# Weight buffers 64 bytes further on in SBUF, activations in place

## Chip, cores and metric

One core of one Trainium2 chip. The metric is the time of one execution on the device in microseconds. "Faster" and "slower" compare medians of several executions.

## What is computed

The reference runs two transformer blocks on a sequence of 512 tokens with a model width of 1024, all in float32.

```python
# first block (16 meta tokens ahead of the 512)
z = rms(h) @ w_in                     # 1024 x 7168: q, k, v, glu, two gates
o = differential attention of 8 heads, block-causal mask
u = silu(layernorm(causal depthwise conv of 31 taps(glu gated)))
m = sigmoid(g_att) * y_att + sigmoid(g_conv) * (u @ w_conv_out)
h = h + m @ w_out
h = h + (silu(gate) * val) @ w_down   # gate, val = conv3(rms(h) @ w_up), 2 x 2816 wide
# second block, two layers
proj = rms(x) @ w_in_2[layer]         # 1024 x 8192
mix  = [gated conv branch (1024), retention of 8 heads (1024)]
x = x + rms(mix @ w_out_2[layer])     # 2048 x 1024
```

Nearly all the arithmetic is matrix products of a weight matrix with the activations.

## The kernel before

Activations live transposed in SBUF: 128 channels on the partitions, tokens along the free axis, one slice for each of the 8 (`KT`) groups of 128 channels. Weights come from memory in chunks of 256 (`CW`) output columns: one chunk is 8 slices of 128 x 256 float32, 1 MB. Two buffers of each kind take turns (`j` = 0, 1).

To keep the accuracy of float32 with operands in the format float32r, every product is made of three. A chunk lands in `raw[j]` (SyncE's `load`, line 257). ScalarE copies it to `w_hi[j]`, rounded (`hi`, line 865). VectorE writes the rest, `raw - w_hi`, to `w_lo[j]` (`lo`, line 1228). The activations have such a pair too: `n_hi`/`n_lo`, `m_hi`/`m_lo`, `u_lo`, `s_hi`/`s_lo`, `x_hi`/`x_lo`. Then TensorE adds up w_hi * x_lo, w_hi * x_hi and w_lo * x_hi over the 8 slices in PSUM.

`tile` (line 390) issues this for 128 output columns. Its matmul (line 406) has the weight slice `w[j][:, k, jj*128:(jj+1)*128]` as stationary operand and the activations as moving operand. With 512 tokens that is one matmul; with more (`T1` = 528 tokens with the meta tokens, `T2` = 514 of them) it is two pieces, 256 columns into one bank and the rest (272 or 258) into the other. The argument `c0` is the column at which the moving operand begins: 0, or `OLD` = 14 where the first block drops 14 of the meta tokens (two groups of projections in the attention stretch, the convolution gate). Each piece loads its weights anew.

In two places the roles are turned, since there tokens are wanted on the partitions. `v_block` (line 509) makes the value of the attention: the stationary operand is a slice of 128 tokens of `n_hi` or `n_lo` that begins at column 16 + 128 q (a fifth block takes columns 0 to 16), the moving operand is `w[0][:, k, :]`, 256 columns (line 520). `head_pair` does the same for the retention: the stationary operand is `s_hi` or `s_lo` from column 128 q, the moving one again `w[0][:, k, :]` (line 751). The first chunk of each retention layer is issued at line 734.

The order of all work is written out by hand for each engine and held together by semaphores. TensorE's order alternates chunks 0 and 1; `lo_full[j]` releases it, and `acc_full` releases ScalarE to overwrite `w_hi[j]`. In the attention stretch slices of later projections (`fill`) are put between the steps of the softmax. TensorE has matmuls of plain float32 as well: scores, transposes through `ident`, the retention sums (line 787).

SBUF tensors are laid out in the order in which the program declares them, each beginning at a multiple of 32 bytes in its partition; those of inner scopes share the bytes behind. The first is `raw0` at byte 16512. The places before the change:

| tensor | byte | modulo 128 | modulo 256 |
|---|---|---|---|
| raw0, raw1 | 16512, 24704 | 0 | 128 |
| w_hi0, w_hi1 | 32896, 41088 | 0 | 128 |
| w_lo0, w_lo1 | 49280, 57472 | 0 | 128 |
| h, par, ident | 65664, 82560, 85120 | 0 | 128 |
| n_hi, n_lo (rows of 2304 bytes) | 101504, 119936 | 0 | 128 |
| m_hi, m_lo (rows of 2304 bytes) | 138368, 156800 | 0 | 128 |
| s_hi, s_lo (rows of 2048 bytes) | 101504, 117888 | 0 | 128 |
| x_hi, x_lo (rows of 2048 bytes) | 134272, 167040 | 0 | 128 |

Of the kernel before, what the change touches and what calls it, by code (L numbers as in the profile page):

```python
# [24 lines left out]
P = 128  # L25
# [62 lines left out]
def build(nc, io, out):  # L88
# [14 lines left out]
    with ctx:  # L103
        def sb(name, shape, dt=fp32, at=None):
            return (at or ctx).enter_context(nc.sbuf_tensor(name, shape, dt))
# [2 lines left out]
            return ctx.enter_context(nc.semaphore(name))  # L108


        raw = [sb(f"raw{j}", [P, KT, CW]) for j in range(2)]
        w_hi = [sb(f"w_hi{j}", [P, KT, CW], f32r) for j in range(2)]
        w_lo = [sb(f"w_lo{j}", [P, KT, CW], f32r) for j in range(2)]
# [22 lines left out]
        head_ms = sb("head_ms", [P, UNITS])  # L136
        lams = sb("lams", [1, 4])
        sub_w = sb("sub_w", [P, 1])
        sb("to_the_phase_of_w", [P, 32])


        area = ExitStack()
# [1719 lines left out]
```

## Time and profile before

| | us |
|---|---|
| median of 3 runs (lowest, highest) | 1958.2 (1957.84, 1959.83) |
| profiled execution | 1962.2 |
| its span, first to last instruction | 1960.4 |
| mean granted TensorE clock | 0.982 |

The profile divides the span into 40 slices of 49 us. The first lines are the busy shares in tenths, then the clock granted to TensorE, and the bandwidth moved:

```profile
PE   6999999999999999999899999999989999999998
DVE  6677897886546546566575554444256555544422
ACT  4224454355333323234422222222232222222222
PEclk7999999999999999999899999999989999999999
DMA  4221111112223222222322323232322323232321
```

PE is TensorE (matmuls), PEld its weight loads, DVE VectorE, ACT ScalarE. The first 45 us are start and first normalisation; the GLU projections run to 152, the attention to 441, the output projections and the feed-forward network to 950, the two retention layers to 1445 and 1940. A matmul's duration in the profile is longer than the distance from its start to the next one's, since matmuls are pipelined.

### The profile page before, as it was taken

How to read it: one execution, taken by the hardware profiler on the slowest of the kernel's cores; microseconds unless marked ns; L12 is line 12 of the kernel's file. 1: busy time of each engine (PE TensorE's matmuls, PEld its weight loads, DVE VectorE, ACT ScalarE, POOL GpSimd, SP SyncE). 2: the span in 40 equal slices, each digit the busy share in tenths (PEclk: the TensorE clock that was granted, in tenths of full speed). 3: DMA queues.
4: the chain of work that ended last, by engine and by line, in shares of the span. 5: the costliest groups of instructions: out<-in, count | busy, mean ns of one | idle time of the engine just before them, and what ended most of it. 6: DMA issues, size and time to landing. Idle time of an engine off the chain costs nothing.

```text
span 1960.4 us, 29930 instructions
## 1 busy us (share of the span) xinstructions
PE 1906.9 (97%) x11809; PEld 1694.7 (86%) x11809; DVE 1142.0 (58%) x1516; ACT 627.5 (32%) x1060; POOL 72.8 (4%) x69
## 2 busy tenths in 40 slices
PE   6999999999999999999899999999989999999998
PEld 5998888889999999899788888888878888888887
DVE  6677897886546546566575554444256555544422
ACT  4224454355333323234422222222232222222222
POOL 2000100110000000000000000000000000000000
PEclk7999999999999999999899999999989999999999
DMA  4221111112223222222322323232322323232321
GB/s 133 89 87 64 65 43 64 64 50 79 87 90 103 80 93 95 98 86 65 97 72 90 94 78 106 87 97 96 106 75 67 94 78 96 86 107 86 104 90 43
DMA packets 159216, 165.86 MB, mean 85 GB/s; under 512 B 2968, under 2 KB 156065, under 8 KB 159154
## 3 DMA queue, kind: packets, MB, share of 16 engines
q1 hardware_dynamic: 156648, 160.73, 26.3%
q10 hardware_dynamic: 2186, 4.20, 0.6%
q8 instruction: 44, 0.72, 0.2%
q14 instruction: 18, 0.15, 0.0%
q0 software_dynamic: 320, 0.07, 0.0%
HBM read 162.88 MB, written 2.10 MB: 84 GB/s over the span
## 4 chain that ended last, share of the span: by engine, by line
issue 50%; PE 41%; DVE 6%; POOL 1%; ACT 1%; DMA 0%; DVEq 0%; POOLq 0%; ACTq 0%
PE acc L406 29%; PE acc L520 3%; PE acc L734 2%; PE acc L751 2%; DVE y L1312 1%; PE tr L787 1%; PE sc L562 1%; DVE ssum L1698 1%; PE sc L773 1%; DVE w_lo L1228 1%; POOL pw L347 0%; PE tr L593 0%; DVE ssum L1276 0%; PE tr L440 0%; PE tr L591 0%
## 5 line engine op out<-in xcount | busy, mean ns | idle before, releaser
L1228 DVE TENSOR_TENSOR w_lo<-raw,w_hi 128x2048 fp32r<-128x2048 f32 x148 | 338.7, 2289 | 157.7 <-ACT w_hi L865 156.2
L865 ACT ACTIVATE w_hi<-raw 128x2048 fp32r<-128x2048 f32 x147 | 280.8, 1910 | 447.9 <-PE acc L406 432.8
L406 PE MATMUL acc<-s_lo,w_hi 128*128 128x512 f32 x848 | 333.0, 393 | 0.0
L406 PE MATMUL acc<-s_hi,w_lo 128*128 128x512 f32 x848 | 330.3, 389 | 0.0
L406 PE MATMUL acc<-s_hi,w_hi 128*128 128x512 f32 x848 | 330.1, 389 | 0.0
L406 PE MATMUL acc<-n_lo,w_hi 128*128 128x256 f32 (+3 forms) x1072 | 259.9, 310 | 6.1 <-DVE n_lo L1256 3.1
L406 PE MATMUL acc<-n_hi,w_hi 128*128 128x256 f32 (+3 forms) x1072 | 250.8, 302 | 0.0
L406 PE MATMUL acc<-n_hi,w_lo 128*128 128x256 f32 (+3 forms) x1072 | 250.6, 302 | 0.0
L406 PEld LDWEIGHTS acc<-n_lo,w_hi 128*128 128x128 f32 x1072 | 172.8, 190 | 29.0 <-issue 16.7
L406 PEld LDWEIGHTS acc<-s_hi,w_lo 128*128 128x128 f32 x848 | 159.2, 188 | 33.2
L406 PEld LDWEIGHTS acc<-s_lo,w_hi 128*128 128x128 f32 x848 | 159.3, 188 | 32.1
L406 PEld LDWEIGHTS acc<-s_hi,w_hi 128*128 128x128 f32 x848 | 159.3, 188 | 32.0
L406 PEld LDWEIGHTS acc<-n_hi,w_lo 128*128 128x128 f32 x1072 | 173.9, 190 | 6.9
L406 PEld LDWEIGHTS acc<-n_hi,w_hi 128*128 128x128 f32 x1072 | 173.8, 190 | 6.6
L406 PE MATMUL acc<-m_hi,w_hi 128*128 128x256 f32 x832 | 167.9, 283 | 0.0
L406 PE MATMUL acc<-m_hi,w_lo 128*128 128x256 f32 x832 | 167.8, 283 | 0.0
L1312 DVE SCALAR_TENSOR_TENSOR y<-u,par,y (+1 forms) x240 | 164.5, 747 | 1.7 <-DVE neg_lam L1361 0.4
L406 PE MATMUL acc<-m_lo,w_hi 128*128 128x256 f32 x704 | 143.5, 285 | 0.8 <-DVE h L1525 0.2
L406 PEld LDWEIGHTS acc<-m_hi,w_lo 128*128 128x128 f32 x832 | 129.1, 190 | 0.0
L406 PEld LDWEIGHTS acc<-m_hi,w_hi 128*128 128x128 f32 x832 | 129.0, 190 | 0.0
L406 PEld LDWEIGHTS acc<-m_lo,w_hi 128*128 128x128 f32 x704 | 109.1, 190 | 3.9 <-DVE z L1545 2.4
L406 PE MATMUL acc<-x_hi,w_lo 128*128 128x512 f32 x256 | 99.6, 389 | 0.0
(274 smaller groups left out, 2619.7 us busy)
## 6 DMA issues: line engine op xcount, KB each, us to landing
raw<-in_w_in SPq DMA_DIRECT2D x92, 1024.0 KB, 5.8
raw<-in_w_up SPq DMA_DIRECT2D x22, 1024.0 KB, 5.1
raw<-in_w_out SPq DMA_DIRECT2D x20, 1024.0 KB, 5.2
raw<-in_w_down SPq DMA_DIRECT2D x8, 1024.0 KB, 5.1
raw<-in_w_conv_out SPq DMA_DIRECT2D x4, 1024.0 KB, 5.3
decay<-in_decay ACTq DMA_DIRECT2D x8, 512.0 KB, 5.3
raw<-in_w_down SPq DMA_DIRECT2D x4, 768.0 KB, 4.8
xs<-in_x SPq DMA_DIRECT2D x4, 512.0 KB, 5.2
```

The source lines that it names most:

```text
L406: last = pe.matmul(acc[jj][:, bank, at_:at_ + n], w[j][:, k, jj * P:(jj + 1) * P], x[:, k0 + k, c:c + n], start=start and k == 0 and p == ...
L520: last = pe.matmul(dst, x[:, k, c:c + m], w[0][:, k, :], start=k == 0 and p == 0, stop=k == KT - 1 and p == 2)
L562: last = pe.matmul(sc[:, m, 0:keys], qs, kT[part, hh, 0:keys], start=True, stop=True)
L734: last = pe.matmul(acc[jj][:, j, :], w[j][:, k, jj * P:(jj + 1) * P], x[:, k, :], start=k == 0 and w is w_hi and x is s_hi, stop=k == KT - ...
L751: last = pe.matmul(acc[jj][:, 0, (q % 2) * CW:(q % 2 + 1) * CW], x[:, k, q * P:(q + 1) * P], w[0][:, k, :], start=k == 0 and p == 0, stop= ...
L773: last = pe.matmul(dst, rk[:, hh, kb * P:(kb + 1) * P], rq[:, hh, kb * P:SEQ], start=True, stop=True)
L787: last = pe.matmul(dst[:, q * P:(q + 1) * P], st[:, c:c + P], rv[:, kb, hh * P:(hh + 1) * P], start=kb == 0, stop=kb == q)
L865: act.activation(w_hi[j][:, :, :], raw[j][:, :, :], ACT.Copy).then_inc(hi_full[j], 1)
L1228: dve.tensor_tensor(w_lo[j][:, :, :], raw[j][:, :, :], w_hi[j][:, :, :].bitcast(fp32), ALU.subtract).then_inc(lo_full[j], 1)
L1312: dve.scalar_tensor_tensor(out=dst, in0=src, scalar=w, in1=dst, op0=ALU.mult, op1=ALU.add).then_inc(s["conv"], 1)
L1698: dve.tensor_reduce(ssum[:, 0:SEQ], h2[:, :, :].rearrange("p t n -> p n t"), AX.X, ALU.add).then_inc(s["hsum"], 1)
```

## The change

A tensor `lead` of 16 floats (64 bytes in each partition) is declared ahead of `raw`, and the pad that stood after `sub_w`, 32 floats, is replaced by one of 16. Neither is read or written. All tensors from `raw0` to `sub_w` move up by 64 bytes; the weight buffers then begin at 64 modulo 128 (192 modulo 256). `n_hi` and everything declared after it stay at their bytes. No instruction is added, taken away or moved.

```diff
+        sb("lead", [P, 16])
         raw = [sb(f"raw{j}", [P, KT, CW]) for j in range(2)]
         w_hi = [sb(f"w_hi{j}", [P, KT, CW], f32r) for j in range(2)]
         w_lo = [sb(f"w_lo{j}", [P, KT, CW], f32r) for j in range(2)]
...
         sub_w = sb("sub_w", [P, 1])
-        sb("to_the_phase_of_w", [P, 32])
+        sb("to_the_phase_of_x", [P, 16])
```

## Rows read from the trace of the kernel before

**Rows 1.** The page: busy us, share of the span, instructions of each engine.

```profile
PE 1906.9 (97%) x11809; PEld 1694.7 (86%) x11809; DVE 1142.0 (58%) x1516; ACT 627.5 (32%) x1060; POOL 72.8 (4%) x69
```

**Rows 2.** Busy time by stage: stretch, length, then each engine's busy us.

```profile
45.00:152.00 107.00, 106.41 (x865) 105.62 (x866) 77.49 (x98) 23.44 (x19) 0.00 (x0) 1.00 0.30 98
152.00:441.00 289.00, 282.24 (x2228) 251.16 (x2228) 236.94 (x454) 136.01 (x444) 34.30 (x12) 1.00 0.17 56
441.00:950.00 509.00, 504.40 (x3669) 478.82 (x3669) 299.59 (x353) 183.63 (x201) 4.82 (x2) 0.99 0.28 89
1000.00:1445.00 445.00, 444.46 (x2184) 373.60 (x2182) 210.07 (x241) 115.77 (x165) 7.35 (x8) 1.00 0.31 93
```

**Rows 3.** Chain that ended last, 1600 to 1960: start, us, what, count.

```profile
1646.47 11.51 PE acc L751 x96
...
1684.04 255.70 PE acc L406 x1128
```

**Rows 4.** Timeline of TensorE, feed-forward, first and last of 37 rows.

```profile
893.12 0.40 PE L406 MATMUL acc<-m_lo,w_hi 128*128 128x256 f32 x2
...
901.76 0.40 PE L406 MATMUL acc<-m_lo,w_hi 128*128 128x256 f32 x2
```

**Rows 5.** Timeline of TensorE, GLU, width T1, first and last of 25 rows.

```profile
59.97 0.41 PE L406 MATMUL acc<-n_hi,w_lo 128*128 128x256 f32 x2
...
65.83 0.40 PE L406 MATMUL acc<-n_hi,w_lo 128*128 128x256 f32 x2
```

**Rows 6.** Timeline of TensorE, from column 14, first and last of 38 rows.

```profile
129.93 0.40 PE L406 MATMUL acc<-n_hi,w_hi 128*128 128x256 f32 x2
...
138.81 0.40 PE L406 MATMUL acc<-n_hi,w_lo 128*128 128x256 f32 x2
```

**Rows 7.** Timeline of TensorE, line 520, first and last of 13 rows.

```profile
156.75 0.28 PE L520 MATMUL acc<-w_hi,n_hi 128*128 128x256 f32 x1
...
158.11 0.28 PE L520 MATMUL acc<-w_hi,n_hi 128*128 128x256 f32 x1
```

**Rows 8.** Groups of matmuls by shape: count, busy us, mean ns of one.

```profile
L406 PE MATMUL acc<-s_hi,w_lo 128*128 128x512 f32 x848 | 330.3, 389 | 0.0
...
L406 PE MATMUL acc<-m_hi,w_hi 128*128 128x258 f32 x416 | 117.3, 282 | 0.0
...
L406 PE MATMUL acc<-x_hi,w_lo 128*128 128x512 f32 x256 | 99.6, 389 | 0.0
...
L406 PE MATMUL acc<-m_lo,w_hi 128*128 128x258 f32 x352 | 99.3, 282 | 0.0
...
L751 PE MATMUL acc<-w_hi,s_hi 128*128 128x256 f32 x256 | 73.6, 288 | 0.0
...
L406 PE MATMUL acc<-n_hi,w_hi 128*128 128x512 f32 x176 | 68.5, 389 | 0.0
...
L406 PE MATMUL acc<-n_hi,w_hi 128*128 128x258 f32 x240 | 68.5, 285 | 0.0
...
L406 PE MATMUL acc<-n_hi,w_hi 128*128 128x272 f32 x208 | 60.1, 289 | 0.0
...
L520 PE MATMUL acc<-w_hi,n_hi 128*128 128x256 f32 x128 | 35.4, 277 | 0.0
...
L406 PE MATMUL acc<-u_lo,w_hi 128*128 128x258 f32 x64 | 18.0, 282 | 0.0
...
L520 PE MATMUL acc<-w_hi,n_hi 128*16 128x256 f32 x32 | 8.8, 276 | 0.0
```

**Rows 9.** The page's groups and DMA issues: mean ns, us to landing.

```profile
L1228 DVE TENSOR_TENSOR w_lo<-raw,w_hi 128x2048 fp32r<-128x2048 f32 x148 | 338.7, 2289 | 157.7 <-ACT w_hi L865 156.2
L865 ACT ACTIVATE w_hi<-raw 128x2048 fp32r<-128x2048 f32 x147 | 280.8, 1910 | 447.9 <-PE acc L406 432.8
...
raw<-in_w_in SPq DMA_DIRECT2D x92, 1024.0 KB, 5.8
```

**Rows 10.** Who waited for whom: us in total, times, longest.

```profile
ACT w_hi L865 <- PE acc L406: 432.8, 71, 10.8
```

## The prediction, made before the changed kernel was run

> **What bounds the kernel now.** I read the busy shares first [rows 1]: TensorE has matmuls in flight for 1906.9 of 1960.4 us. Only 53.5 us of the span are without one. The table by stage [rows 2] says the same more sharply: between 1000 and 1445 us TensorE is busy for 444.46 of 445 us while VectorE is busy for 210 and ScalarE for 116. The second retention layer repeats this. The feed-forward stretch (441 to 950) stands at 504.4 of 509, the GLU stretch (45 to 152) at 106.4 of 107. Only in the attention stretch (152 to 441) does VectorE come near, with 236.9 of 289. So the time of this kernel is the number of matmuls times their pace, and any edit that leaves the pace alone is worth little.
>
> The change adds no instruction, no wait and no transfer. It moves addresses. The question is therefore whether the pace of a matmul depends on where its operands begin, and the trace holds a natural experiment on that.
>
> **The pace, read from the trace.** The durations that the profile gives a matmul overlap their neighbours; the pace is the distance between starts. At a granted clock of 1.00 (the 2.4 GHz level) 512 columns stream in 213.3 ns and 256 in 106.7 ns. What lies above is paid per matmul:
> - 512 columns, weights stationary: 255.70 us for 1128 matmuls, 226.7 ns each [rows 3], 13.4 ns above.
> - Pieces of 256 and 258 over `m_hi`/`m_lo`: 36 pairs from 893.12 to 901.76, 240.0 ns a pair [rows 4]. Streaming is 214.2, so 12.9 ns above for each matmul.
> - Pieces of 256 and 272 over `n_hi`/`n_lo` (width T1): 24 pairs from 59.97 to 65.83, 244.2 ns a pair, streaming 220.0, so 12.1 each [rows 5].
> - Pieces of 256 and 258 over `n_hi`/`n_lo` that begin at column 14, 56 bytes in: 37 pairs from 129.93 to 138.81, 240.0 ns, 12.9 each [rows 6].
> - Line 751 (the retention value, activation slice stationary, weights moving, 256 columns): 11.51 us for 96, 119.9 ns, 13.2 above [rows 3].
> - Line 520 (the attention value, again activation slice stationary, weights moving, 256 columns): 12 steps from 156.75 to 158.11, 113.3 ns, 6.6 above [rows 7].
>
> The last two are the same matmul in shape and in moving operand (`w_hi[0]`, `w_lo[0]`). What differs is the stationary slice. Line 751 takes `s_hi[:, k, q*128:...]`, whose byte address is a multiple of 128. Line 520 takes `n_hi[:, k, 16+q*128:...]`: the META offset of 16 floats puts it 64 bytes past a multiple of 128. Every weight slice of line 406 is at present a multiple of 128 (`w_hi0` is at byte 32896 = 257*128, slices step by 512) and so is every activation tensor it streams, except where column 14 is added. So all matmuls with a stationary operand at phase 0 pay about 13 ns, and the one group with the stationary operand at phase 64 and the moving one at phase 0 pays half. After the change line 406 has just that arrangement, in absolute bytes too: stationary at 192 modulo 256, moving at 128 modulo 256.
>
> Two things in the rows weaken this. The 16-column loads of line 520 (fifth block, columns 0 to 16) begin at phase 0 and its matmuls show the same duration as the 128-column ones, 276 against 277 ns [rows 8]; a short load may simply be free, but it may also be that `n` as stationary operand is cheap for another reason: its rows are 2304 bytes apart, those of `s` 2048. And a moving operand 56 bytes in [rows 6] gains nothing over one at 0, although its distance to the weights is then nearly 64 as well. So it may be the phase of the stationary operand alone that counts.
>
> The Trainium skill speaks against any effect. Its page "TensorE: Matmul & The Clock Gate", section "Step-by-step: what each phase is for", says that TensorE has two independent read ports of SBUF and that loading the next tile's weights takes no bandwidth from the running matmul; by that a shift of 64 bytes changes nothing and the time stays. Rows 3 against rows 7, 119.9 against 113.3 ns for one shape, are not explained by it.
>
> **The change part by part.** Moving `lead` in ahead of `raw0` and shrinking the pad after `sub_w` from 128 to 64 bytes moves raw, `w_hi`, `w_lo`, `h`, `par`, `ident`, the statistics tiles and `pw` up by 64 bytes. `n_hi` stays at byte 101504, with everything behind it.
>
> (a) Line 406 and weights at phase 64, activations at phase 0. With 512 columns: 3 passes of 848, 256 and 176 matmuls [rows 8], together 3840, each from 13.4 to 6.6 above streaming, 6.8 ns: 26.1 us. Pieces of 256/258 from column 0: over `m` 416+416+352 pairs, over `u_lo` 64, over `n` in the output projection 2*2*2*8 = 64 for each of three passes, together 1440 pairs or 2880 matmuls, 6.3 ns each: 18.1 us. Width T1: 208 pairs in each of three passes [rows 8], 1248 matmuls, from 12.1 to 6.6, 5.5 ns: 6.9 us. Sum 51.1 us. The 144 matmuls of line 734 are left out (1.0 us).
>
> (b) Pieces from column 14: 240-64 = 176 pairs a pass, 1056 matmuls. Stationary 64, moving 56. If the stationary phase alone counts, 6.3 ns each, a gain of 6.7 us; if the distance counts, they stay about equal, 0.
>
> (c) Line 520: stationary stays at 64, moving goes to 64. 384 matmuls with 128-column loads [rows 8]. 0, or a loss of 6.6 ns each, 2.5 us.
>
> (d) Line 751: stationary stays at 0, moving goes to 64. 768 matmuls [rows 8]. 0, or a gain of 6.6 ns each, 5.1 us.
>
> (b) to (d) come as one of two sets: +6.7 for "stationary phase", +2.6 for "distance". I take the middle, 4.6, and keep both ends. Gross 55.7 us.
>
> (e) What does not pass through. In the attention stretch the matmuls between the softmax steps are filler, and VectorE is busy 82% of it. The gain there is 384 matmuls of width T1 (2.1 us) and up to 768 from column 14 (4.8 us); I count half of it lost, 2 us. At the start of the kernel, at the two layer starts and at its end the saved time of a few matmuls meets a chain of statistics that is no shorter; I take 2.5 us. Net 51 us.
>
> (f) The weight path. A 1 MB load lands in 5.8 us, is copied by ScalarE in 1.91 and split by VectorE in 2.29 us [rows 9]. A chunk of 48 matmuls of 512 columns lasts 48*226.7 = 10.9 us, or 10.6 after, and the two conversions take 4.2 of it, the load having landed a chunk earlier. The copy waits for TensorE for 432.8 us in all [rows 10], so it is early, not late. Its cover holds: were the load to take twice as long for its new phase, or both conversions 10% more (0.4 us), nothing of it would show. Their operands all move together, so I take 0. If that cover were gone, 0.4 us for each of 147 chunks would be 59 us.
>
> (g) float32 matmuls (transposes, scores) keep stream and operands, apart from `ident`, `nf` and `rb`, which move 64 bytes; 0, with an end of 2 us either way.
>
> **The sum.** The profiled execution took 1962.2 us (span 1960.4). 1962.2-51 = 1911.2. The median of the runs is 4.0 us under the profiled one, so the forecast is 1907 us.
>
> **The rivals.** (1) No effect: the 113.3 ns of line 520 belong to the pitch of `n` or to its role, not to its phase. Then the time is 1958, within a microsecond or two. For it: the 16-column loads, the 56-byte rows and the port rule. (2) Only 256-column matmuls gain, since only those were seen fast; with 512 columns the pace stays at 226.7. Then (a) is 18.1+6.9 = 25.0 us, with 4.6 from (b) to (d) and 4.5 lost in (e) 25.1 net: 1933. (3) Slower: a 512-byte weight slice from a multiple of 128 covers four blocks of 128 bytes, from 64 past it five. If each block read costs a pause, 13.4 ns at four is 3.35 a block, and the fifth adds 3.35 ns to 7968+1056 = 9024 matmuls: 30 us, 1988. It decides from the point where line 520, whose slices lie across five blocks already, owes its pace to something else that hides the fifth; its 113.3 ns speaks against this directly.
>
> **How the numbers follow.** The likeliest case 0.66; no effect 0.17; half 0.06; slower 0.11. The likeliest case's own range is 1896 to 1925: its low end takes all of +6.7, no loss in (e) and (g) for it (1958.2-51.1-6.7-1.0-2 = 1897, and one more for the reading of the paces), its high end lets three fifths of the gross 55.7 through (33). To leave out no more than 2 in 10 the range must also take in the no-effect case, so 1896 to 1961. About 0.2% (4 us) is what a measurement of this kernel can tell from no change. Faster 0.72, same 0.17, slower 0.11.
>
> **What would show it.** In the changed kernel the long run of line 406 at the end should show 1128 matmuls in about 248 us (219.9 ns each), a pair over `m` about 227.4 ns. If lines 520 and 751 keep 113.3 and 119.9 while the column-14 pairs fall to 227, the stationary phase counts; if 520 rises to 120 and 751 falls to 113, the distance does. If the pace of line 406 stays at 226.7, the prediction is wrong at its root, and nothing else in the kernel could bring 50 us. If the pace falls but the time does not, the waits on VectorE's `w_lo` and softmax tiles should have grown.

## The result: slower, and the working part of the forecast had the wrong sign

| | before | after |
|---|---|---|
| median of 3 runs (lowest, highest), us | 1958.2 (1957.84, 1959.83) | 1975.94 (1975.91, 1978.34) |
| profiled execution, us | 1962.2 | 1978.34 |
| its span, us | 1960.4 | 1976.5 |
| mean granted TensorE clock | 0.982 | 0.985 |

The ratio after/before is 1.0089, 95% interval 1.0074 to 1.0103. The forecast was 1907 us in a range of 1896 to 1961. The kernel did not get 51 us shorter, it got 18 us longer.

### The profile after

The busy line of the changed kernel's page:

```profile
PE 1923.3 (97%) x11809; PEld 1686.5 (85%) x11809; DVE 1141.9 (58%) x1516; ACT 627.7 (32%) x1060; POOL 72.7 (4%) x69
```

Against [rows 1] the instruction counts are the same on every engine. VectorE, ScalarE and GpSimd are busy for the same time within 0.2 us. TensorE alone changed: 1906.9 to 1923.3 us, 16.4 more, where the span grew by 16.1 (its weight loads, PEld, which run beside the matmuls, are busy 8.2 us less). Its mean granted clock is no lower, 0.985 against 0.982. So no wait was added; the matmuls themselves come at another pace.

The busy time by stage, to be laid beside [rows 2] (stretch, length, then each engine's busy us, granted clock, DMA share, GB/s):

```profile
45.00:152.00 107.00, 106.50 (x878) 105.72 (x879) 78.48 (x100) 25.23 (x22) 0.00 (x0) 1.00 0.30 99
152.00:444.00 292.00, 284.85 (x2227) 253.68 (x2227) 237.12 (x452) 135.82 (x443) 34.26 (x12) 1.00 0.18 58
444.00:950.00 506.00, 500.32 (x3662) 471.71 (x3661) 299.31 (x354) 183.67 (x202) 4.82 (x2) 0.99 0.28 90
1007.00:1455.00 448.00, 446.15 (x2146) 367.06 (x2145) 207.33 (x238) 114.94 (x164) 8.05 (x9) 1.00 0.30 90
```

The GLU stretch holds 878 matmuls in 107 us where it held 865: a little faster. The retention stretch holds 2146 in 448 us where it held 2184 in 445: slower. The two signs live in one kernel, and what separates them is the width of the matmul.

The chain that ended last gives the two long runs that answer to [rows 3]:

```profile
1654.72 11.31 PE acc L752 x96
...
1692.49 263.19 PE acc L407 x1128
```

Lines are one higher than before (line 406 is now 407). The 1128 matmuls of 512 columns take 263.19 us instead of 255.70: 233.3 ns each instead of 226.7. The forecast wanted 248. The 96 matmuls of the retention value take 11.31 instead of 11.51: 117.8 ns instead of 119.9.

The narrow ones, from TensorE's timeline. Each group of rows is read as in the prediction, first start to last start: pairs over `m` (42 steps of two pieces), then width T1 (25 steps of two), then from column 14 (41 steps of two), then line 521, the old 520 (33 steps of one):

```profile
895.89 0.40 PE L407 MATMUL acc<-m_hi,w_lo 128*128 128x256 f32 x2
...
905.79 0.40 PE L407 MATMUL acc<-m_hi,w_lo 128*128 128x256 f32 x2
...
59.81 0.40 PE L407 MATMUL acc<-n_lo,w_hi 128*128 128x256 f32 x2
...
65.81 0.40 PE L407 MATMUL acc<-n_hi,w_hi 128*128 128x256 f32 x2
...
130.91 0.40 PE L407 MATMUL acc<-n_hi,w_lo 128*128 128x256 f32 x2
...
140.79 0.40 PE L407 MATMUL acc<-n_hi,w_hi 128*128 128x256 f32 x2
...
155.84 0.28 PE L521 MATMUL acc<-w_lo,n_hi 128*128 128x256 f32 x1
...
159.80 0.28 PE L521 MATMUL acc<-w_lo,n_hi 128*128 128x256 f32 x1
```

From here on I write the places of a matmul as D, the byte at which the stationary operand begins minus that of the moving one, modulo 256 (so -64 and 192 are the same place), and "over" for what a matmul takes above its number of columns divided by 2.4 per ns, as in the prediction.

| matmuls | count | D before, after | over before | over after | in all, us |
|---|---|---|---|---|---|
| 512 columns, lines 406 and 734 | 3984 | 0, +64 | 13.4 | 20.0 | +26.3 |
| pieces 256/258 from column 0 | 2880 | 0, +64 | 12.9 | 10.75 | -6.2 |
| pieces 256/272 (T1) | 1248 | 0, +64 | 12.1 | 10.0 | -2.6 |
| pieces from column 14 | 1056 | -56, +8 | 12.9 | 13.4 | +0.5 |
| line 520, attention value | 384 | +64, 0 | 6.6 | 13.3 | +2.6 |
| line 751, retention value | 768 | 0, -64 | 13.2 | 11.1 | -1.6 |

Before's numbers are those of [rows 3 to 7]; after's are the rows above (for the pairs over `m`: 9.90 us/42 = 235.7 ns, less 214.2, halved). That 256 is enough as a modulus can be seen in the timeline that the rows over `m` come from. From one slice to the next the weights go on by 1024 bytes and `m` by 2304, so D runs through different multiples of 256, and still every pair takes 0.23 or 0.24 us. The sum is +19.0 us where the span grew by 16.1 and the median by 17.7. The whole effect is in the pace, and six groups account for it within 3 us; the rest was not taken apart.

### The profile page after: what moved, and what is told of

It is laid out like the page before. It is cut to its first block, busy times and chain, and to the rows that moved or that the text cites. A ratio compares the mean times of both kernels' runs of the same rounds, so it can differ in the third digit from the quotient of the medians.

```text
span 1976.5 us, 29930 instructions
## 1 busy us (share of the span) xinstructions
PE 1923.3 (97%) x11809; PEld 1686.5 (85%) x11809; DVE 1141.9 (58%) x1516; ACT 627.7 (32%) x1060; POOL 72.7 (4%) x69
## 3 DMA queue, kind: packets, MB, share of 16 engines
q1 hardware_dynamic: 156648, 160.73, 26.1%
## 4 chain that ended last, share of the span: by engine, by line
issue 50%; PE 42%; DVE 5%; POOL 1%; ACT 1%; DMA 0%; DVEq 0%; POOLq 0%; ACTq 0%
PE acc L407 30%; PE acc L521 3%; PE acc L735 2%; PE acc L752 2%; DVE y L1313 1%; PE tr L788 1%; PE sc L563 1%; DVE ssum L1699 1%; PE sc L774 1%; POOL pw L348 0%; PE tr L594 0%; DVE ssum L1277 0%; PE tr L441 0%; PE tr L592 0%; DVE w_lo L1229 0%
## 5 line engine op out<-in xcount | busy, mean ns | idle before, releaser
L866 ACT ACTIVATE w_hi<-raw 128x2048 fp32r<-128x2048 f32 x147 | 280.9, 1911 | 454.8 <-PE acc L407 439.6
L407 PE MATMUL acc<-s_lo,w_hi 128*128 128x512 f32 x848 | 338.0, 399 | 0.0
L407 PE MATMUL acc<-s_hi,w_hi 128*128 128x512 f32 x848 | 335.1, 395 | 0.0
L407 PE MATMUL acc<-s_hi,w_lo 128*128 128x512 f32 x848 | 335.1, 395 | 0.0
L407 PE MATMUL acc<-x_lo,w_hi 128*128 128x512 f32 x256 | 101.2, 396 | 0.0
```

The source lines that it names most:

```text
L407: last = pe.matmul(acc[jj][:, bank, at_:at_ + n], w[j][:, k, jj * P:(jj + 1) * P], x[:, k0 + k, c:c + n], start=start and k == 0 and p == ...
L866: act.activation(w_hi[j][:, :, :], raw[j][:, :, :], ACT.Copy).then_inc(hi_full[j], 1)
```

## Experiments

Two theories stood against each other once the result was known. (A) The pace depends on the distance D alone. (B) It depends on where an operand lies: the weights' slices now lie across five blocks of 128 bytes (rival 3), or only the stationary operand's own place counts. A third (C) was that the neighbours in memory count: `raw`, `h` and the rest moved too.

Each experiment stands beside fresh executions of the kernel before on its own chip: their median was 1959.76 us for the first three and 1958.67 us for the last four. The kernels of bare matmuls were executed once each, on three chips; the granted clock was 1.00 in all the stretches read from them.

### Everything by 64 bytes

```diff
+        sb("lead", [P, 16])
         raw = [sb(f"raw{j}", [P, KT, CW]) for j in range(2)]
...
         sb("to_the_phase_of_w", [P, 32])
```

> Weights and activations both 64 bytes further on than in the kernel before, so each begins at phase 192 modulo 256 and their distance is 0 again. If only the distance between stationary and moving operand sets the pace: 512-column matmuls of line 406 back to 226.7 ns a step, line 520 113.3, line 751 120, time 1958 us. If the byte at which the stationary slice begins counts by itself: 512 columns stay at 233.4, time near 1976. If the moved statistics tiles, h or ident cause the loss: also near 1976.

Measured: 1960.17 us against 1959.76 of the kernel before on the same chip, ratio 1.0004 (0.9994 to 1.0014). The chain that ended last:

```profile
1646.66 11.51 PE acc L752 x96
...
1684.23 255.73 PE acc L407 x1128
```

The weight slices lie across five blocks here as they do after the change, and still 512 columns take 226.7 ns. Rival 3's mechanism falls, and so does "the stationary operand's place alone". What the change altered is the distance between the two.

### The activations by 64 bytes, the weights in place

```diff
-        sb("to_the_phase_of_w", [P, 32])
+        sb("to_the_phase_of_w", [P, 48])
```

> Only the activations move, 64 bytes further on; the weights stay at phase 128 modulo 256. Distance as in the change but with the other sign. If the distance counts modulo 128: 512 columns at 233.4 ns, line 520 (stationary now at 0, moving at 128 modulo 256) at 120, line 751 at 113 to 118, time 1974 to 1978. If the weights' own phase is what costs: 512 columns at 226.7 and the time 1958.

Measured: 1962.58 us against 1959.76, ratio 1.0019 (1.0009 to 1.0029).

```profile
1644.64 10.90 PE acc L751 x96
...
1681.72 258.21 PE acc L406 x1128
```

The distance is -64 for line 406 and +64 for line 751. 512 columns: 228.9 ns, over 15.6, not 20. Line 751: 113.5 ns, over 7. An even period of 128 bytes, in which -64 and +64 are one place, would have made this kernel as slow as the change. It is not, so the sign of the distance counts, and the period is not 128. Line 751 at +64 also shows that the 113.3 ns of line 520 had nothing to do with the pitch of `n`: `s` has it too at that distance. And line 520 lost it in the changed kernel, where its pitch and its role were what they had been. Both halves of rival 1 fall.

### The other tensors by 64 bytes, weights and activations in place

```diff
         w_lo = [sb(f"w_lo{j}", [P, KT, CW], f32r) for j in range(2)]
+        sb("gap", [P, 16])
...
-        sb("to_the_phase_of_w", [P, 32])
+        sb("to_the_phase_of_w", [P, 16])
```

> The tiles between the weights and the activations (h, par, ident, statistics, pw) move 64 bytes, as in the change; weights and activations stay. Theory of the distance: every float32r pace as before, 1958 us within 2. Rival, that the moved tiles bring the loss through VectorE or the plain float32 matmuls: up to 1976.

Measured: 1958.76 us against 1959.76, ratio 0.9998 (0.9988 to 1.0008); the same run of 1128 matmuls:

```profile
1682.03 255.70 PE acc L407 x1128
```

`h`, `par`, `ident` and the statistics tiles do not matter. (C) falls for them; `raw` was moved only together with the weights, and with both operands moved it cost nothing.

### Bare matmuls over the whole range of distances

This kernel computes nothing of the model. ScalarE writes two float32r tiles once, then TensorE runs 24 matmuls of each kind, each with a new stationary slice, and the output is zeros.

```diff
+            for i in range(24):  # s 64 m 0 n (512,)
+                k = i % 4
+                last = pe.matmul(acc[i // 4 % 2][:, 0, 0:512], wt[:, k * 256 + 16:k * 256 + 144],
+                                 mv[:, k * 512 + 0:k * 512 + 0 + 512], start=True, stop=True)
```

> No model any more, a bench: runs of 24 float32r matmuls with 128-column stationary slices, one source line for each pair of start bytes and width; the output is zeros. Stationary start from 0 to 240 bytes in steps of 16 against a moving start at 0, 512 and 256 columns; four starts for 256/258, 256/272 and 384 columns; four cases with the moving operand at 64 bytes. Distance theory: equal starts give 226.7 ns at 512 and 120 at 256 wherever both lie; 64 apart gives 233.4 at 512 and 113.3 at 256. Rival (the stationary start alone): moving both by 64 bytes gives the same as moving the stationary one. Rival (it takes the other engines' traffic to show): all starts alike, about 216 and 109 ns.

TensorE's timeline. The distance between the starts of two groups, divided by 24, is the pace of the first. The source lines follow in steps of 3 for every 16 bytes of D: L59 is D = 0, L71 is +64, with 512 columns; L107 is 0 and L119 +64 with 256. L191 has both operands at 64, L194 the moving one alone.

```profile
42.22 5.60 PE L59 MATMUL acc<-mv,wt 128*128 128x512 f32 x24
47.66 5.61 PE L62 MATMUL acc<-mv,wt 128*128 128x512 f32 x24
...
64.30 5.76 PE L71 MATMUL acc<-mv,wt 128*128 128x512 f32 x24
69.89 5.72 PE L74 MATMUL acc<-mv,wt 128*128 128x512 f32 x24
...
131.13 3.03 PE L107 MATMUL acc<-mv,wt 128*128 128x256 f32 x24
134.00 3.01 PE L110 MATMUL acc<-mv,wt 128*128 128x256 f32 x24
...
142.51 2.89 PE L119 MATMUL acc<-mv,wt 128*128 128x256 f32 x24
145.23 3.02 PE L122 MATMUL acc<-mv,wt 128*128 128x256 f32 x24
...
216.52 5.61 PE L191 MATMUL acc<-mv,wt 128*128 128x512 f32 x24
221.97 5.66 PE L194 MATMUL acc<-mv,wt 128*128 128x512 f32 x24
```

At D = 0, 5.44/24 = 226.7 ns; at +64, 5.59/24 = 232.9; both at 64, 5.45/24 = 227.1. With 256 columns: 2.87/24 = 119.6 at D = 0, 2.72/24 = 113.3 at +64. The paces of the model kernel (226.7 and 233.3, 120.0 and 113.3) come back in a kernel without any other work. So no contention with VectorE, ScalarE or DMA is needed for them. Group by group in this way (a hundredth of a microsecond in a start is 0.4 ns):

| D, bytes | 0 | 16 | 32 | 64 | 96 | 128 | 160 | 192 | 208 | 240 |
|---|---|---|---|---|---|---|---|---|---|---|
| 512 columns, ns | 226.7 | 227.1 | 232.9 | 232.9 | 234.2 | 233.8 | 232.9 | 228.8 | 233.3 | 227.5 |

The cheap places for 512 columns are few here: 0, 16 and 240, with 192 in between (the -64 of the experiment with the activations, 228.9 there). With 256 columns +64 is the cheapest of the sweep, 113.3, and 192 gives 117.5. So D = +64 is the best place for one width and among the worst for the other. The last group of this kernel (256 columns, stationary at 0, moving at 64) shows that 256 columns can run at 113 ns at D = -64 too: its 24 matmuls took 2.88 us in all, as those of L119 did (2.89), not the 2.99 of D = 192 in the sweep.

### Width, load and absolute place

Bare matmuls again, with zeros as output.

```diff
+            for i in range(24):
+                c, k, n = 0, (i % 4), 240
+                last = pe.matmul(acc[i // 4 % 2][0:128, 0, 0:n], wt[:, k * 256 + 0:k * 256 + 128],
+                                 mv[:, k * 512 + 0 + c:k * 512 + 0 + c + n], start=True, stop=True)
```

> Bench as before, 136 runs of 24 matmuls; output zeros. Theory: what is paid above streaming comes from the loading of the next weights while a matmul streams, and depends on how the two reads lie to each other. Then slices of 16 columns bring 512 columns with the stationary start 64 bytes on from 20 to 7 ns above streaming or less, and slices of 32, 64, 96 columns lie between; a sweep of widths at equal starts gives paces that are multiples of 13.33 ns (32 columns), at 64 bytes apart multiples plus 6.67 up to some width and a step more beyond it. Rival: the cost is the matmul's own, and the number of stationary columns changes nothing. The distance theory further expects that moving both starts by 64, 128 or 192 bytes leaves each pace; a rival is that byte 0, 128 or the row pitch count too (256 columns with the stationary start 64 bytes behind: 6.7 above streaming in one place, 11.1 in another).

The timeline, first by width at D = 0; then 512 columns at D = +64 with 128 stationary columns, and at D = 0 with 16; then pairs that keep the distance at +64 and at -64 and move both operands (L234 stationary at 128, moving at 64; L237 64 and 128; L240 192 and 128; L243 128 and 192):

```profile
53.36 2.85 PE L66 MATMUL acc<-mv,wt 128*128 128x240 f32 x24
56.05 3.03 PE L69 MATMUL acc<-mv,wt 128*128 128x256 f32 x24
...
206.27 5.76 PE L183 MATMUL acc<-mv,wt 128*128 128x512 f32 x24
211.87 5.66 PE L186 MATMUL acc<-mv,wt 128*16 128x512 f32 x24
217.36 5.72 PE L189 MATMUL acc<-mv,wt 128*32 128x512 f32 x24
...
278.20 5.75 PE L234 MATMUL acc<-mv,wt 128*128 128x512 f32 x24
283.79 5.67 PE L237 MATMUL acc<-mv,wt 128*128 128x512 f32 x24
289.30 5.76 PE L240 MATMUL acc<-mv,wt 128*128 128x512 f32 x24
294.89 5.67 PE L243 MATMUL acc<-mv,wt 128*128 128x512 f32 x24
```

With 512 columns, wherever the two lie, +64 gives 5.59 or 5.60/24 = 233 ns and -64 gives 5.51/24 = 229.6. The absolute place has no say, the sign has. For 256 columns this kernel can't tell the sign: the same moves gave 117.9 or 113.3 ns, at +64 and at -64 alike.

A stationary slice of 16 columns does not make 512 columns cheap. At D = 0 it takes 5.49/24 = 228.8 ns against 227.9 for 128 columns in this kernel; at +64 it takes 231.2 against 233.3, so 17.9 over where the theory wanted 7 or less. With 256 columns at D = 0 it does help: 116.7 ns for 16 columns, 113.7 for 32 and 113.8 for 64, 119.2 for 128. So the cost over streaming is not simply the reading of the weights, amount by amount, and the idea that it is proportional to the load falls. At 224 and at 240 columns the pace is the same, 2.69/24 = 112.1 ns, as at 192 and 208 (111.7 and 112.1). All of these load 128 columns anew; whether the load is what holds them there was not tested with narrower slices.

The sweep of widths shows where the sign of the effect turns. Paces in ns, read from the timeline as above:

| columns | 256 | 272 | 288 | 304 | 336 | 384 | 416 | 432 | 448 | 464 | 480 | 496 | 512 |
|---|---|---|---|---|---|---|---|---|---|---|---|---|---|
| D = 0 | 119.2 | 125.4 | 131.7 | 137.9 | 153.3 | 173.3 | 187.9 | 195.4 | 203.3 | 208.8 | 216.7 | 223.3 | 227.9 |
| D = +64 | 117.5 | 123.8 | 132.9 | 138.8 | 155.8 | 177.1 | 186.7 | 193.3 | 202.1 | 213.8 | 215.8 | 226.7 | 233.3 |

The gain of +64 ends between 272 and 288 columns, comes back by 1 to 2 ns from 416 to 448 columns, and 512 columns have the largest loss. (The widths left out of the table fit in between.) Differences of a few ns between the two ends are to be read with care, since 384 columns at +64 took 173.3 to 177.1 ns in different places of these kernels. The sweep also refutes the theory of steps of 13.33 ns: 125.4, 137.9 and 187.9 are no multiples of it.

The good place for 512 columns is narrow. With the stationary start 4 or 8 bytes past D = 0 the same kernel took 232.1 ns, and 8 bytes short of it 233.8.

The same kernel gave a warning. D = 16 took 233.3 ns here, after pairs of 256 and 272, and 227.1 in the first kernel of bare matmuls, after D = 0; 256 columns at D = +64 took 117.9 or 113.3. The pace is not a function of the operands alone.

### The weights by 128 bytes

```diff
+        sb("lead", [P, 32])
...
-        sb("to_the_phase_of_w", [P, 32])
```

> Weights 128 bytes further on instead of 64, activations in place. Distance counted modulo 256 (bench: 20.2 ns above streaming at 512 columns, 14.2 for 256/258, 13.2 for 256/272): +27, +3.7 and +1.4 us, line 520 +1.6, about 1992. Distance counted modulo 128: as before, 1958.

Measured: 1981.29 us against 1958.67, ratio 1.0112 (1.0096 to 1.0128). The run of 1128 matmuls:

```profile
1697.42 262.13 PE acc L406 x1128
```

Slower even than the change, by some 5 us (22.6 above the kernel before, where the change was 17.7), since now the 256-column work gains little (pairs over `m` 12.0 over, on the mean of all of them) and the 512-column work loses all the same (232.4 ns). That D = 0 and D = 128 differ shows once more that the period is above 128. The forecast of 1992 was too high by 11 us. Some 4 of them are the 512 columns, which settled at 232.4 ns and not at the 233.5 of the forecast (1.1 ns for each of 3984). The pairs over `m` are another 5 (2368 matmuls at 12.0 over, not 14.2).

These pairs are the clearest sign of two paces inside the model kernel. Of the same instructions on the same operands, 30 pairs from 739.73 to 746.83 us take 236.7 ns each and 25 pairs from 896.76 to 902.80 take 241.6.

### The change in halves

The first block alone at +64: the change, with the retention's tensors moved on as well.

```diff
+        sb("lead", [P, 16])
...
-        sb("to_the_phase_of_w", [P, 32])
+        sb("to_the_phase_of_w", [P, 16])
...
+            sb("back", [P, 16], fp32, c)
             s_hi = sb("s_hi", [P, KT, SEQ], f32r, c)
```

(`ob`, where the second block ends, is moved on in the same way.)

> The change in the first block alone: weights 64 bytes on, n and m where they were, but s and x (second block) moved 64 bytes with the weights. Narrow pieces 2880 times -2.2 ns, width T1 1248 times -1.9, line 520 384 times +6.0, the 528 of 512 columns in the down projection +6.4: -3.0 us, 1955 to 1956. If the narrow pieces did not gain: 1964.

The second block alone at +64: the change, with `n_hi` and what follows moved on, in the first block only.

```diff
+        sb("lead", [P, 16])
...
-        sb("to_the_phase_of_w", [P, 32])
+        sb("to_the_phase_of_w", [P, 16])
...
+            sb("back", [P, 16], fp32, area)
             n_hi = sb("n_hi", [P, KT, ROW], f32r, area)
```

> The change in the second block alone: weights 64 bytes on, n and m moved with them, s and x where they were. 3456 matmuls of 512 columns times +6.5 ns, line 751 768 times -2.1: +20.9 us, about 1979, above the changed kernel itself.

Measured, both against 1958.67 us: the first block alone 1957.59, ratio 0.9992 (0.9983 to 1.0001); the second alone 1979.13, ratio 1.0107 (1.0089 to 1.0125). Their effects are -1.1 and +20.5 us, together 19.4, where the change as a whole cost 17.7. The chains, of the second block alone and then of the first alone:

```profile
1656.05 11.31 PE acc L753 x96
...
1693.82 263.19 PE acc L408 x1128
```

```profile
1680.31 255.73 PE acc L409 x1128
```

The second block carries the whole loss: it consists almost only of matmuls of 512 columns. In the first block the narrow pieces gain, and its own matmuls of 512 columns (`n`, 176 in each of three passes) and line 520 give most of that back: by the table above -6.2 and -2.6 against +3.5 and +2.6 us, and +0.5 for column 14, together -2.2. The 1.1 us of the first block are less than the 3 expected and lie within what the measurement can tell from nothing.

### Only the feed-forward's activations at the distance that suits them

```diff
+                sb("apart", [P, 48], fp32, a)
                 m_hi = sb("m_hi", [P, KT, ROW], f32r, a)
```

> Weights and all else as before; only m_hi and m_lo move (192 bytes on), so that the weights lie 64 bytes ahead of them modulo 256. All their matmuls are pieces of 256 and 258 columns. Distance theory with the paces of the changed kernel: 2368 matmuls at 10.7 instead of 12.9 ns above streaming, 5.2 us less, 1953 to 1954. Rival, that the gain of the narrow pieces seen in the changed kernel came with something else that moved: no difference.

48 floats put `m_hi` and `m_lo` 192 bytes on, so that the weights lie +64 from them, and only from them. Measured: 1954.35 us against 1958.67, ratio 0.9976 (0.9967 to 0.9986). It is the fastest kernel of the study, and the gain of 4.3 us (2.7 to 6.5 by the interval) is the one the pace gives: the timeline shows 43 steps of two pieces in 10.13 us, 235.6 ns a pair instead of 240.0 [rows 4], and 1184 pairs by 4.4 ns are 5.2 us.

```profile
892.73 0.40 PE L407 MATMUL acc<-m_hi,w_hi 128*128 128x256 f32 x2
...
902.86 0.40 PE L407 MATMUL acc<-m_hi,w_lo 128*128 128x256 f32 x2
```

### What went before, and bfloat16

The pairs over `m` now run at D = +64 and yet show 10.8 over, not the 6.6 that line 520 showed at the same distance. This kernel of bare matmuls (zeros as output) ran 40 of 256 columns at D = +64 each time after 12 of another width, and also bfloat16 tiles.

```diff
+            for i in range(12):
+                c, k, n = 0, (i % 4), 320
+                last = pe.matmul(acc[i // 4 % 2][0:128, 0, 0:n], wt[:, k * 256 + 16:k * 256 + 144],
+                                 mv[:, k * 512 + 0 + c:k * 512 + 0 + c + n], start=True, stop=True)
+            for i in range(40):
+                c, k, n = 0, (i % 4), 256
+                last = pe.matmul(acc[i // 4 % 2][0:128, 0, 0:n], wt[:, k * 256 + 16:k * 256 + 144],
+                                 mv[:, k * 512 + 0 + c:k * 512 + 0 + c + n], start=True, stop=True)
```

> Bench, output zeros. First part: 40 matmuls of 256 columns with the stationary start 64 bytes on, each run after 12 of another width. If the pace has more than one stable state, chosen by how the run begins, some runs stay at 113.3 and others at 117.8 ns for the same operands; if it is fixed by the operands, all are alike. 512 columns: 226.7 at equal starts and 233.3 at 64, whatever came before. Last part: bfloat16 operands, half the bytes a column. If the cost is the reading of 4-byte operands at full rate, they run at 213.3 plus 2 to 3 ns at every start; if it is a matter of weight load against matmul in general, the start shows there too.

The timeline: L62 follows matmuls of 512 columns, L80 follows 320; L251 and L254 are 512 columns in bfloat16 at two distances.

```profile
49.09 4.87 PE L62 MATMUL acc<-mv,wt 128*128 128x256 f32 x40
53.80 2.26 PE L65 MATMUL acc<-mv,wt 128*128 128x384 f32 x12
...
68.49 4.71 PE L80 MATMUL acc<-mv,wt 128*128 128x256 f32 x40
73.04 1.65 PE L83 MATMUL acc<-mv,wt 128*128 128x272 f32 x12
...
324.27 8.81 PE L251 MATMUL acc<-mb,wb 128*128 128x512 bf16 x40
332.92 8.80 PE L254 MATMUL acc<-mb,wb 128*128 128x512 bf16 x40
```

The same 40 instructions on the same operands take 4.71/40 = 117.8 ns each when a run of 512 columns went before, and 4.55/40 = 113.8 after 320 columns. After 384, 256 and 272 columns it was 117.8 as well, after 448 and 258 it was 113.3 and 113.5, after 128 it was 114.8: no order by width. So at D = +64 there are two paces for 256 columns. That what went before chooses between them is the likeliest reading, since nothing else was varied, but each width was put ahead only once. At D = 0 there is one pace, 119.7 to 120.0 (121.0 after 128 columns). With 512 columns D = 0 and +64 have one pace each, 227.5 to 227.7 and 233.5 after 256, 384 and 272 columns (229.5 and 234.5 after 128). D = 128 had two, 232.2 or 232.3 after 384 and 256 and 233.5 after 272, the first being what the kernel with the weights moved by 128 bytes settled at; D = 16 had two as well.

The pairs fit this only in part. As bare matmuls after a run of 512, pairs of 256 and 258 took 119.6 ns a piece at D = 0 and 120.8 at +64, no gain. In the first kernel of bare matmuls, where such a pair loads two different slices and follows other narrow matmuls, they took 120.0 and 117.5, which is the gain of 2.1 in the model kernel and a little more. Which of the two differences decides was not separated.

In bfloat16 all four distances tried give 216 ns for 512 columns and 109 for 256, 2 to 3 ns over streaming. The rule of the Trainium skill that the prediction weighed is that TensorE has two independent read ports, so that loading the next weights takes no bandwidth from the running matmul (page "TensorE: Matmul & The Clock Gate", section "Step-by-step: what each phase is for"). Taken as the prediction took it, that a shift then changes nothing, it agrees with these rows and not with the float32r ones, 226.7 against 233.3 ns for one shape. Whether bandwidth is what the float32r matmuls lose, no run here shows.

## Why the prediction was wrong, point by point

**The bound: right.** The time is the number of matmuls times their pace. The span grew by 16.1 us and TensorE's busy time by 16.4; no other engine moved by more than 0.2.

**The pace depends on where operands lie: right.** It does, and by the distance: line 520 rose to 120.0 ns and line 751 fell, which is the set that the prediction called "distance". Line 751 fell only to 117.8, since its distance became -64; at +64, with the activations moved, it was at 113.5. With both operands moved nothing changed, so "stationary phase alone" is out, and with the 17.7 us of the change "no effect" (rival 1) as well.

**(a), 512 columns: the step that failed.** The prediction had one fast row, 256 columns at +64 [rows 7], and gave its 6.8 ns to 3840 matmuls of 512 columns. No row of before showed a 512-column matmul at any distance but 0. Measured there: +6.6 ns each, where -6.8 was forecast. That is -26.1 forecast and, for the same 3840, +25.3 measured: 51.4 of the 68.9 us that separate 1907 from 1975.94. The unknown had been given a worst case of no gain (rival 2), with no room for a loss: a bound on both sides of zero would have let 512 columns lose what 256 gain. Why they lose it stays open.

**(a), pieces of 256 to 272: right in sign, mis-sized.** -18.1 and -6.9 us were forecast, -6.2 and -2.6 came: another 16.2 us. The pace of line 520 was taken for a constant of the distance. It is one of two paces at that distance, and the pairs settled at 117.8 ns a piece (235.7/2). Why pairs of 256 and 258 choose the slower one is not settled.

**(b) to (d):** -4.6 forecast, +1.5 measured by the table. The pieces from column 14 went from D = -56 to +8 and stood still; the matmuls of line 520 lost their 2.6 us, as the loss end of (c) had it.

**(e)** has no meaning with the sign reversed: nothing was saved that could be lost, and its 4.5 us come off the miss. The four terms, 51.4 + 16.2 + 6.1 - 4.5 = 69.2, make the miss of 68.9. The agreement is closer than the paces are known: with the 1.0 us of line 734, which the forecast left out, the table adds up to 1.3 us more than the median moved.

**(f), the weights' path: right.** The load, copy and split kept their cover. The copy is as early as it was:

```profile
ACT w_hi L866 <- PE acc L407: 439.6, 71, 10.6
```

439.6 us of waiting for TensorE where it was 432.8 [rows 10]. **(g)** was right at 0: with `ident`, `nf` and `rb` moved alone the time stayed (ratio 0.9998).

**The rivals.** Rival 3, slower, was right in sign with a mechanism that the first experiment refutes; it had put 30 us on the blocks that a slice covers, for every width alike. Rival 2 had the right division, by width, and the wrong value for the wider half: 0 where it was +25. The 16-column rows that weakened the case [rows 8] stood at D = 0 and were fast. In the kernel before 23 steps of them take 2.61 us, 113.5 ns each, where the 128-column loads of the same line take 120.0 at D = 0 in the changed kernel:

```profile
164.43 0.28 PE L520 MATMUL acc<-w_hi,n_lo 128*16 128x256 f32 x1
...
167.04 0.28 PE L520 MATMUL acc<-w_lo,n_hi 128*16 128x256 f32 x1
```

Bare matmuls of 256 columns gain from a narrow slice at D = 0 too (116.7 against 119.2 ns), so the prediction's first reading, a short load, was the better one.

## What to carry to other kernels

In float32r, the bytes between the start of the stationary operand and that of the moving one are a parameter of each matmul: place 512-column products at exactly 0 modulo 256 (4 bytes off cost 4 to 5 ns, nearly as much as 64), and try +64 for those near 256 columns, tensor by tensor (here 0.24% for moving `m` alone). A pace seen at one width is evidence for that width only; before carrying it over, run two dozen bare matmuls of the other width behind the work that precedes them in the kernel, or give the term a bound on both sides of zero. When a move of addresses costs time, move both operands together first: if that is free, as here, the distance is the cause and can be set back without undoing the change.

## What the runs showed of the hardware that was not expected

- The same shape in float32r at the 2.4 GHz level takes 226.7 or 233.3 ns for 512 columns and 120.0, 117.8 or 113.3 for 256, by the distance modulo 256 (and for some distances by something else, probably what ran before). For 512 columns the absolute place had no say in any pair tried. 226.7 is 17 times 13.33 ns and 120.0 is 9 times, but 125.4 ns at 272 columns and 187.9 at 416 fit no such step.
- For 256 columns at +64 two paces exist for the same instructions, 117.8 and 113.8 ns on the mean of 40; the only thing varied was the run before them. Pairs of 256 and 258 at D = 128 have two paces as well, 236.7 and 241.6 ns, within one execution of the model kernel.
- With 512 columns at D = 0 a stationary slice of 16 columns saved nothing against 128 (228.8 against 227.9 ns), and matmuls of 192 to 240 columns all took 112 ns.
- bfloat16 shows none of it: 216 and 109 ns at every distance tried.
- Open: why the gain of +64 turns into a loss between 272 and 288 columns, and which of its two paces a run at +64 falls into within the kernel.
